# First two FFN inputs: input rewritten with its root at round three, second slot pair of every second round as block product too

## The reference

```python
def rms_norm(x, g):
    y = xf * lax.rsqrt(jnp.mean(xf * xf, axis=-1, keepdims=True) + RMS_EPS)
    return (y * g.astype(jnp.float32)).astype(x.dtype)

def swiglu_ffn(h, w_ffn_in, w_ffn_out):
    g, u = jnp.split(h @ w_ffn_in, 2, axis=-1)
    return (jax.nn.silu(g) * u) @ w_ffn_out

f = swiglu_ffn(rms_norm(h, norm_ffn_pre[layer]), w_ffn_in[layer], w_ffn_out[layer])
```

## Time and profile before

| | |
|---|---|
| median of 3 executions | 2221.7 us |
| profiled execution | 2220.7 us, its span 2218.9 us |
| TensorE busy | 2203.3 us |
| VectorE busy | 1633.6 us |
| ScalarE busy | 1097.6 us |
| DMA | mean 99 GB/s |
| granted TensorE clock over the span | 0.999 |

### The profile page before, as it was taken

How to read it: one execution, slowest core, us unless ns; L and a number is a source line. 1 busy time by engine, 2 the same in 40 slices (tenths; PEclk the granted TensorE clock), 3 DMA queues, 4 the chain that set the end, 5 groups by cost and what they waited for, 6 DMA issues and landing times.

```text
span 2218.9 us, 39662 instructions
## 1 busy us (share of the span) xinstructions
PE 2203.3 (99%) x15576; PEld 1942.5 (88%) x15576; DVE 1633.6 (74%) x2486; ACT 1097.6 (49%) x1724; POOL 13.2 (1%) x22
## 2 busy tenths in 40 slices
PE   9999999999999999999999999999999999999998
PEld 7788898989988989989988877899888888898898
DVE  7675777686877776687757665788896875888895
ACT  7454634453526644454542364544553784544543
POOL 0000000001000000000000000000000000000000
PEclk9999999999999999999999999999999999999999
DMA  4212323333472233323232112333233203323322
GB/s 170 71 64 89 96 101 104 104 102 103 148 209 90 89 102 104 104 96 105 90 118 78 58 49 77 104 104 113 93 97 105 79 30 105 105 96 102 105 96 96
DMA packets 81897, 219.08 MB, mean 99 GB/s; under 512 B 11552, under 2 KB 30440, under 8 KB 81760
## 3 DMA queue, kind: packets, MB, share of 16 engines
q1 hardware_dynamic: 72656, 206.02, 28.2%
q10 hardware_dynamic: 7952, 9.47, 1.4%
q0 software_dynamic: 1152, 1.67, 0.3%
HBM read 212.78 MB, written 4.34 MB: 98 GB/s over the span
## 4 chain that ended last, share of the span: by engine, by line
PE 96%; DVE 1%; ACT 1%; issue 0%; DMA 0%; ACTq 0%; SPq 0%; DVEq 0%
PE bank L650 17%; PE bank L651 16%; PE bank L652 16%; PE bank L863 5%; PE bank L866 5%; PE bank L867 5%; PE bank L1021 5%; PE bank L1022 5%; PE bank L1023 5%; PE bank L980 2%; PE bank L979 2%; PE bank L978 2%; PE bank L672 2%; PE bank L673 1%; PE bank L676 1%; PE bank L1343 1%
## 5 line engine op out<-in xcount | busy, mean ns | idle before, releaser
L650 PE MATMUL bank<-u_hi,w_hi 128*128 128x512 f32 (+1 forms) x1466 | 544.8, 372 | 1.9 <-ACT av L1963 1.2
L651 PE MATMUL bank<-u_lo,w_hi 128*128 128x512 f32 (+1 forms) x1466 | 542.3, 370 | 0.0
L652 PE MATMUL bank<-u_hi,w_lo 128*128 128x512 f32 (+1 forms) x1466 | 542.0, 370 | 0.0
L1537 ACT ACTIVATE w_hi<-raw 128x1024 fp32r<-128x1024 f32 x344 | 360.9, 1054 | 328.0 <-DMA raw<-weights_dram 175.3
L2319 DVE TENSOR_TENSOR w_lo<-raw,w_hi 128x1024 fp32r<-128x1024 f32 x344 | 417.9, 1220 | 94.8 <-ACT w_hi L1537 89.8
L650 PEld LDWEIGHTS bank<-u_hi,w_hi 128*128 128x128 f32 x1466 | 275.3, 188 | 50.8 <-issue 1.9
L652 PEld LDWEIGHTS bank<-u_hi,w_lo 128*128 128x128 f32 x1466 | 275.4, 188 | 48.0
L651 PEld LDWEIGHTS bank<-u_lo,w_hi 128*128 128x128 f32 x1466 | 275.3, 188 | 45.5 <-issue 0.2
L1021 PE MATMUL bank<-hid_hi,w_hi 128*128 128x256 f32 (+1 forms) x616 | 202.1, 328 | 0.0
L1022 PE MATMUL bank<-hid_lo,w_hi 128*128 128x256 f32 (+1 forms) x616 | 201.9, 328 | 0.0
L1023 PE MATMUL bank<-hid_hi,w_lo 128*128 128x256 f32 (+1 forms) x616 | 201.8, 328 | 0.0
(11 more groups left out here) (424 smaller groups left out, 4729.6 us busy)
## 6 DMA issues: line engine op xcount, KB each, us to landing
raw<-weights_dram SPq DMA_DIRECT2D x363, 512.0 KB, 3.3
bz<-gated_dram SPq DMA_DIRECT2D x30, 268.0 KB, 4.7
raw<-weights_dram ACTq DMA_DIRECT2D x13, 512.0 KB, 4.1
gated_dram<-bz SPq DMA_DIRECT2D x8, 274.0 KB, 4.4
h<-x_t_dram SPq DMA_DIRECT2D x8, 256.0 KB, 5.6
raw<-weights_dram SPq DMA_DIRECT2D x4, 256.0 KB, 5.0
out_dram<-m SPq DMA_DIRECT2D x4, 256.0 KB, 2.4
out_dram<-m ACTq DMA_DIRECT2D x4, 256.0 KB, 2.5
```

What stands on the lines that cost most here:

```text
L650: pe.matmul(out, wh, xh, start=start, stop=False)
L651: pe.matmul(out, wh, xl, start=False, stop=False)
L652: return pe.matmul(out, wl, xh, start=False, stop=stop)
L1537: act.activation(slot_of(w_hi, s, i), slot_of(raw, s, i), ACT.Copy).then_inc(hi_ready, 1)
```

## The change

**In the FFNs of layers a and b:**
- `PAIRED`: in rounds 4, 6 and 8 the second pair becomes a block product too. Three pairs a layer.
- The operands of that second block product (weight sums and their low parts) lie in parts of `hid_hi`, `sum_32`, `hid_lo` and `hid_32` that are free at the time; those of the first stay in `s_hi` and `s_lo`. Its banks are 2, 3 and 5; its kept intermediates lie in `ut`.
- `plain` now contains the root: h times gain times `rs`. VectorE makes it (`plain_input`, in three portions of 3, 2 and 3 tiles around pair (1, 0)), no longer ScalarE.
- During the last chunk of round 2 (`last_unscaled`) TensorE signals each k tile, ScalarE rewrites `u_hi` from `plain` and VectorE `u_lo`. TensorE waits for `u_lo`'s tile 1 before the turn matmul of round 3, for tile 4 before the second quarter, for tile 8 before the third.
- From round 3 on nothing is multiplied by `rs`: a plain pair's silu is read by ScalarE straight from the bank, `keep_pair` is one instruction.
- The hardware loop over rounds becomes written-out code on TensorE, ScalarE and VectorE. The high and low parts of the first ten hidden chunks are made behind the last silu instead of before it.

**In layer a's mixer:** the first three conv chunks wait for 1, 2 and 4 emptied banks instead of 4 each.

Layers c and d compute the same in the same order.

The diff, cut to its core:

```diff
+PAIRED = {"a": (4, 6, 8), "b": (4, 6, 8), "c": (), "d": ()}
...
+                def last_unscaled(i):
+
+                    j, out = s0 + RING * i + 3, hidden_bank(l, i, 1, 1)[:, :]
+                    pe.wait_ge(ht_ready, SCALED[l] + 2 * i)
+                    pe.wait_ge(w_ready, j + 1)
+                    for k in range(KC):
+                        last = product(out, weight(w_hi, j, k), weight(w_lo, j, k), u_hi[:, k, :], u_lo[:, k, :], k == 0, k == KC - 1)
+                        if k < KC - 1:
+                            last.then_inc(quad_full, 1)
+                    last.then_inc(slot_done, 1)
...
+                def paired_quad(i, b):
...
+                    pe.wait_ge(w_ready, s + 2)
+                    if (i, b) == (QUAD_FROM[l], 0):
+                        pe.wait_ge(u_ready, SPLIT[f"{l}_fnorm"] + 1)
+                    if b == 0:
+                        pe.matmul(v, weight(w_hi, s, 0), u_hi[:, 0, HALVED_AT:HALVED_AT + HT], start=True, stop=True, skip_group_check=True)
+                    quarter(y, of_slot(1, 4), of_sum(Q_S4), True).then_inc(quad_full, 1)
+                    if (i, b) == (QUAD_FROM[l], 0):
+                        pe.wait_ge(u_ready, SPLIT[f"{l}_fnorm"] + 4)
+                    quarter(z, of_slot(0, 0), of_input(0, 0), True).then_inc(quad_full, 1)
+                    if (i, b) == (QUAD_FROM[l], 0):
+                        pe.wait_ge(u_ready, SPLIT[f"{l}_fnorm"] + KC)
+                    quarter(v, of_slot(0, 4), of_input(4, 0), True)
+                    pe.wait_ge(mix_low, mix_count(MIX_LOW, 2, l, i, b, 2))
+                    quarter(w, of_mixed(Q_S1), of_sum(Q_S1), True, slots_read=True).then_inc(quad_full, 1)
...
                 elif n < 3:
-                    pe.wait_ge(a_evac, TT)
+                    pe.wait_ge(a_evac, (1, 2, TT)[n])
...
ACT:
+                        for k in range(KC):
+                            if k < KC - 1:
+                                act.wait_ge(quad_full, FREED[l] - KC + 1 + 6 * QUAD[l] + k + 1)
+                            else:
+                                act.wait_ge(slot_done, s0 + n)
+                            act.activation(u_hi[:, k, :], plain[:, k, :], ACT.Copy).then_inc(uh_ready, 1)
...
DVE:
+                def plain_input(chunks):
+
+                    for c in chunks:
+                        dve.wait_ge(rs_ready, RS[f"{l}_fpre"] + 1)
+                        dve.scalar_tensor_tensor(out=plain[:, c, :], in0=h[:, c, :], scalar=pre_gain(f"{l}_fpre", c), in1=rs[:, :],
+                                                 op0=ALU.mult, op1=ALU.mult).then_inc(v_ready, 1)
...
+                    if at:
+                        keep_pair(*items[at - 1])
+                    if quad_next:
+                        mix_pair(*following)
+                    low_part(s + 2)
+                    (half_low if quad_next else lambda s, i: low_part(s))(s + 3, 0)
+                    if is_quad(l, i, b):
+                        dve.wait_ge(quad_full, FREED[l] + quad_count(6, l, i, b, 5))
+                        dve.wait_ge(snap_ready, quad_count(4, l, i, b, 4))
+                        dve.tensor_tensor(gconv[:, b, :], pair_kept(b)[:, 1, :], bank[2 * b][:, :], ALU.add).then_inc(row_sum, 1)
+                    if quad_next:
+                        low_pair(*following)
```

More of the change, by code:

```diff
@@ L194, in weight_row, with paired_items, is_quad, quad_before @@
     return s
-def quad_slot(s):
-    return any(SLOT[f"{l}_ffn_in"] + RING * QUAD_FROM[l] <= s < SLOT[f"{l}_ffn_out"] and (s - SLOT[f"{l}_ffn_in"]) % RING < 2
-               for l in QUAD_FROM)
+def paired_items(l):
+    return [(i, b) for i in range(QUAD_FROM[l], ROUNDS) for b in range(2)]
+def is_quad(l, i, b):
+    return b == 0 or i in PAIRED[l]
+def quad_before(l, i, b):
+    found = [n for n in range(QUAD_FROM[l], i) if is_quad(l, n, b)]
+    return found[-1] if found else None
+def quad_number(l, i, b):
+    return [item for item in paired_items(l) if is_quad(l, *item)].index((i, b))
+def quad_slot(s):
+    for l in QUAD_FROM:
+        n = s - SLOT[f"{l}_ffn_in"]
+        if RING * QUAD_FROM[l] <= n < 2 * FC:
+            return is_quad(l, n // RING, n % RING // 2)
+    return False
 def slot_at(s, i=0):
@@ new lines, in paired_round @@
+                def paired_round(i, b):
+                    if is_quad(l, i, b):
+                        paired_quad(i, b)
+                        return
+                    s = s0 + RING * i + 2 * b
+                    if is_quad(l, i - 1, b):
+                        pe.wait_ge(row_sum, quad_count(2, l, i - 1, b, 2))
+                    else:
+                        pe.wait_ge(gate_ready, HID[l] + 2 * i)
+                    chunk(s, 0, hidden_bank(l, i, b, 0)[:, :], u_hi, u_lo)
+                    if not is_quad(l, i - 1, b):
+                        pe.wait_ge(t2_ready, HID[l] + 2 * i)
+                    chunk(s + 1, 0, hidden_bank(l, i, b, 1)[:, :], u_hi, u_lo)
@@ new lines, in low_pair @@
+                def low_pair(i, b):
+                    for q in (Q_S1, Q_S2):
+                        n = 8 if b == 0 else 4 if q == Q_S1 else 12
+                        at = 2 if b == 0 and q == Q_S2 else q
+                        dve.wait_ge(mix_high, mix_count(MIX, 2, l, i, b, q + 1))
+                        dve.tensor_tensor(pair_low(b, at, True, n=n), pair_low(b, at, False, n=n), pair_high(b, at, n=n).bitcast(F32),
+                                          ALU.subtract).then_inc(mix_low, 1)
@@ L2620, in rounds @@
                     low_part(s0 + RING + 2, i)
-                def gate(i, b, *fill):
-                    scaled_gate(i, b)
-                    if fill:
-                        fill[0]()
-                    if second is not None:
-                        taps(i, b)
-                    for more in fill[1:]:
-                        more()
-                def kept(i, b):
-                    keep_hidden(i, b, hidden_bank(l, i, b, 1)[:, :])
-                if l in "cd":
-                    low_sum(f"{l}_fpre")
-                    first_lows(s0)
@@ L2721, in feed_forward, with gate, kept @@
                     split_low(ROUNDS - 1)
+                def gate(i, b, *fill):
+                    scaled_gate(i, b)
+                    if fill:
+                        fill[0]()
+                    if second is not None:
+                        taps(i, b)
+                    for more in fill[1:]:
+                        more()
+                def kept(i, b):
+                    keep_hidden(i, b, hidden_bank(l, i, b, 1)[:, :])
+                if l in "cd":
+                    low_sum(f"{l}_fpre")
+                    first_lows(s0)
```

355 lines of the change are left out of this document (271 added, 84 removed).

## The result

| | before | after |
|---|---|---|
| median, 22 executions each | 2220.9 us (2219.6 to 2222.5) | 2223.9 us (2221.9 to 2226.6) |
| ratio | | 1.0013, 95% interval 1.0007 to 1.0019 |
| profiled execution (its span) | 2220.7 (2218.9) us | 2226.6 (2224.8) us |
| TensorE, VectorE, ScalarE busy | 2203.3, 1633.6, 1097.6 us | 2201.8, 1648.9, 1113.0 us |

The changed kernel takes 3.0 us more. That is a small loss clear of the noise (the interval lies above 1), under the 0.2% that the forecast took as its measure, and inside its range. The forecast was 1.1 us more.

What follows compares the result with a forecast made beforehand. TensorE was taken as the bound. Against the profiled 2220.7 us: -8.2 for block products, -1.2 for the mixer wait, +10.5 for the FFN openings, so +1.1; as a median 2222.8 us, 8-in-10 range 2215.5 to 2227.5.

Steps and rivals of the forecast that it cites:

- What bounds: Whole kernel: TensorE, busy 99% of the span; only removed matmuls or a wait put before TensorE move the time.
- gains 1 and 2: Six new FFN block products save 1.37 us each, 8.2 us; the finer wait in the first mixer saves 1.2 us.
- Rounds 4, 6, 8 costed at nothing: FFN rounds with two block products: VectorE's idle time hides the added work, no TensorE wait, 0 us.
- Rival B: Rounds 4, 6, 8: slot 19 lands late, TensorE waits 1.8 us six times; +10.8 us, 2233.6; chance 0.12.
- Cost at the opening: FFN opening, layers a and b: 16 added VectorE instructions make TensorE wait; 5.2 us a layer, 10.5 us for two.
- From there to 286.30 VectorE has no wait, so lateness stays: FFN opening after gate (1,1): VectorE's 2.91 us of lateness carries on to low part 9 and later work.
- rival D: FFN opening: TensorE's clock falls to 1.2 GHz after 2 us waits, one chunk 5.4 us longer; +21.8 us, 2244.6; chance 0.03.
- The waits on u_lo: First block product of round 3: TensorE waits 1.9 us before the turn matmul, 0.3 and 1.0 before later quarters.
- The signs of being wrong: Changed profile: TensorE waits under 5 us in sum, waits before (4,1), (6,1), (8,1), or a block product over 9.6 us.
- A: FFN opening: VectorE's added work costs less; 2216.3 us with only the first wait, 2212.3 without any; chance 0.20.
- C: New block products run slower with weight sums in hid_hi and hid_32, saving nothing; +8.2 us, 2231.0; chance 0.03.
- Granted clock 1.00 throughout: Expected sign in the changed profile: TensorE's granted clock never falls from 1.00.

Runs made afterwards that it cites:

- experiment 2: Changed kernel with no second pair as block product, rewritten input kept; 12.7 us above the kernel before, ratio 1.0059.
- experiment 4: Changed kernel with the second pair of every round from 4 to 8 as block product (10 instead of 6); ratio 0.9998 to the kernel before.
- experiment 1: Kernel before with only the change's finer wait in layer a's mixer; 1.2 us under the kernel before, ratio 0.9996.
- experiment 8: Kernel of 7 with the remaining half of the mixed weights' low part behind u_lo, ScalarE's high part likewise behind u_hi; 2210.2 us, ratio 0.9947 to the kernel before.
- experiment 3: Changed kernel with 8 small matmuls on TensorE ahead of value chunk (2,0), layers a and b; ratio 1.0007, 1.3 us above the kernel before.
- experiment 9: Kernel of experiment 8 with round 3's second pair as block product too (12 instead of 10); 2213.3 us, ratio 0.9964 to the kernel before.
- 5: Changed kernel with high parts 8 and 9 ahead of the silus, low part 9 ahead of gate (1,1), layers a and b; 2221.05 us, ratio 0.9997 to before.
- 6: Kernel of 5 with two low parts of sums and half the mixed weights' low part moved behind u_lo; 2216.7 us, ratio 0.9978 to the kernel before.
- 7: Kernel of 6 with the second pair of every round from 4 to 8 as block product; 2211.9 us, ratio 0.9956 to the kernel before.

## Why the prediction was right, and where a term was off

- **What bounds, gains 1 and 2**: right. TensorE's starts give 1.37 us for each of six block products; experiments 2 and 4 show them apart. The mixer gives 1.2 us by the medians of experiment 1 and 1.5 by the starts: the forecast took the idle time of 1.24 us for the whole loss, and its upper bound of 1.24 was too low.
- **Rounds 4, 6, 8 costed at nothing**: right. Three block products in 28.83 us without a wait; even ten instead of six (experiment 4) need nothing more. Rival B's place was checked with a heavier load than the change has and doesn't decide.
- **Cost at the opening**: right in mechanism, too small by the clock: 5.2 us a layer forecast and 6.25 measured. The price of an added input piece (0.67) held, that of a u_lo piece (0.60) too (4.90 us for eight, experiment 8); the three rows before low part 9 came within 0.05 us. The sentence "From there to 286.30 VectorE has no wait, so lateness stays" doesn't hold in the changed kernel: VectorE waits 1.02 us for the value chunk (2,0). But it held wherever the clock stayed up. With the gap filled (experiment 3) and in layer b of experiment 2 TensorE starts that chunk just as late, but VectorE doesn't wait for it, and the opening costs 5.10 and 5.34, against the forecast's 5.24. So the term that was missing is the clock, put at nothing in rival D; VectorE's wait comes with it.
- **The waits on u_lo**: forecast 1.9, 0.3 and 1.0; they were 0.9 and 0.8, and none before the second quarter, because TensorE itself arrived 1.8 us later (289.9, one step of 0.23 behind its last matmul, instead of 288.1), some 1.5 of it for the clock. The time of the third quarter is what counts: 294.2 forecast, 295.1 measured.
- **Rival D, the clock**: dismissed too easily. I took the wait of 1.24 us in the earlier trace rows as the nearest row for one of 2.0; the clock does fall behind 1.94 us, in both layers of the profiled execution. The Trainium skill, "TensorE: Matmul & The Clock Gate", section "Why this matters for your kernels", warns of the half clock behind idle gaps between bursts of matmuls, but of gaps longer than the 1.94 us here. The traces don't bear out that line from either side: the clock fell behind five of six waits of 1.93 to 1.96 us and stayed up behind one of 3.27 (experiment 9). What the fall cost was also mis-sized, the other way: eight slow matmuls, 1.5 us at TensorE and 1.0 to 1.15 us at the end of the opening, and not a whole chunk's 5.4. Had D been booked with the measured size, the forecast would have been +3.4 rather than +1.1 (twice 1.15); the measured value is +3.0. How many of the 22 executions had the fall in both layers isn't known; the profiled one was the slowest.
- **The signs of being wrong**: TensorE's waits in the openings sum to 7.2 us by the profile, over the 5 of A. The three block products in 28.83 us hold two turn matmuls of 0.12, so one takes 9.53 without, and C's 9.6 isn't reached. "Granted clock 1.00 throughout" was wrong.
- **Rival A** (the opening cheaper) and **C** (block products that don't pay) have nothing for them in the runs. Experiments 5, 6 and 8 show what A took for given and the change doesn't do: the same instructions, in another order, cost 0.3 to 0.6 us.

**Still open.** The medians of the changed kernel and of the experiments all lie above what the stage sums give, by 0.2 us (changed kernel) to 2.9 (7); for 8: 1.5 + 10 x 1.37 - 0.8 = 14.4 due, 11.9 measured. Most sums lie within the intervals, those of 2 and 7 at the edge and those of 5 and 6 just past it, but all have one sign. One part is seen in all ten traces: the first 28 us run 0.2 to 1.2 us longer than in the trace of the kernel before, in experiment 1 with the same code. In the trace of 8 another 2.0 us lie in layer b's mixer, between 589 and 763 us of the kernel before, where no code changed. I see two parts there, neither explained: a wait of TensorE, for which the profile shows no releaser, in front of the conv's small matmuls, 0.8 us before, 1.1 after and 2.0 in 8; and the pace below.

## What to carry to other kernels

When a change adds work to an engine that others wait for, price its queue by position: list for each added or displaced instruction the moment at which its reader wants it, and put last what is wanted last. Here the same 16 instructions, with those around them, cost 6.3 us a layer in the order of their making (1.0 to 1.15 of it by the clock) and 0.3 to 0.6 in the order of their use, and the change went from 0.13% slower to 0.53% faster (with four more block products). And when a change puts a new wait in front of TensorE, book the clock behind it as a term with a chance of its own: a row for a shorter wait doesn't tell.

## What was not expected of the hardware

- **A short stretch at the half clock, and no sure sign of it.** These are the waits of TensorE of 1.2 us and more in all eleven traces, and the granted clock behind them:

| clock behind the wait | waits in us (kernel, place) |
|---|---|
| stays at 1.00 | 1.24 (before, mixer), 1.40 and 1.40 (3), 1.31 (2, in front of u_lo), 1.44 (7), 1.80 and 1.79 (5), 1.93 (2, layer b), 1.98 (8, layer b's mixer), 3.27 (9, layer a) |
| falls to 0.50 | 1.93 (2, layer a), 1.93 and 1.96 (4), 1.94 and 1.94 (changed), 3.02 (9, layer b), 3.13 (2, layer c) |

  So it never fell behind a wait of 1.80 us or less and fell behind seven of the ten longer ones, but not by their order: 3.27 us left it up, 1.93 did both in one trace. It can set in with the first matmul or some matmuls later (after five at full pace in the changed kernel, layer b), and it was back at 1.00 each time with TensorE at work. With eight small matmuls in the gap (16 records, experiment 3) it stayed at 1.00 in both layers.
- **Two paces of the same matmul.** A matmul of 256 columns follows another after 0.1133 us in some stretches and 0.1177 in others, at a granted clock of 1.00, with the same code: the 147 matmuls behind 224.8 us took 0.1134 each before and 0.1177 after, 0.63 us in all, and 147 at 571 us took 0.1178 in both kernels. Experiment 1, whose code is the same there as well, took 0.1135 at the first place and 0.1178 at the second. So profiles of the same code differ by some tenths of a microsecond at a place; I found no cause.
